# Softmax attention scores of a two-layer decoder: float32 products replaced by three products of high and low parts

## What is computed

```
qb = q.reshape(B, N, C, Hkv, G, d)              # C = 128 tokens, N = 4 blocks, d = 64
k2 = concatenate([previous key block, own key block])
scores = einsum('bnikgd,bnjkd->bkgnij', qb, k2) * d ** -0.5
logits = concatenate([where(band, scores, -inf), sink]); p = softmax(logits)
```

## Time and profile before

| | us |
|---|---|
| median of 3 runs | 2451.79 |
| lowest, highest run | 2450.35, 2451.99 |
| the profiled execution's own time | 2451.35 |
| its span in the trace | 2449.6 |

### The profile page before, as it was taken

The page is one execution under the profiler, slowest core; times in us unless marked ns, Lnnn a source line. Parts: engine busy times, 40 slices in busy tenths (PEclk is TensorE's granted clock), DMA queues, the critical chain, the costliest instruction groups (busy, mean ns, idle before and its releaser), DMA issues.

```text
span 2449.6 us, 33981 instructions
## 1 busy us (share of the span) xinstructions
PE 2422.6 (99%) x11352; PEld 1982.7 (81%) x11352; DVE 1477.2 (60%) x2263; ACT 869.6 (36%) x1359; POOL 210.5 (9%) x159
## 2 busy tenths in 40 slices
PE   7999999999999999999999999999999999999998
PEld 5888887877788888888888888787778888888887
DVE  3777779677744477433477677877775446533332
ACT  4222223555422342223332222345653223421232
POOL 0023012000003000010300000200100111000001
PEclk9999999999999999999999999999999999999999
DMA  7666664322235336443446566532222343332332
GB/s 265 191 191 189 189 182 142 97 69 60 67 103 148 103 112 197 121 123 104 116 120 191 178 197 198 164 118 80 67 60 78 112 147 102 93 109 82 98 103 82
DMA packets 505534, 315.20 MB, mean 129 GB/s; under 512 B 9256, under 2 KB 497016, under 8 KB 504824
## 3 DMA queue, kind: packets, MB, share of 16 engines
q1 hardware_dynamic: 437456, 246.86, 34.4%
q10 hardware_dynamic: 68008, 67.48, 8.8%
HBM read 308.02 MB, written 6.29 MB: 128 GB/s over the span
## 4 chain that ended last, share of the span: by engine, by line
PE 95%; DVE 3%; issue 1%; DMA 0%; ACT 0%; DVEq 0%; SPq 0%; ACTq 0%
PE ps_proj L1657 28%; PE ps_proj L1659 28%; PE ps_proj L1658 28%; PE ps_mid L1826 1%; PE ps_o L1844 1%; PE ps_mid L1874 1%; PE ps_mid L1875 1%; PE ps_mid L1876 1%; DVE sb_scratch L993 1%; PE ps_mid L1919 1%; PE ps_mid L1833 1%; DVE sb_w_lo L981 1%; PE ps_mid L1659 0%; PE ps_mid L1657 0%; PE ps_mid L1658 0%
## 5 line engine op out<-in xcount | busy, mean ns | idle before, releaser
L1657 PE MATMUL ps_proj<-sb_a_hi,sb_w_hi 128*128 128x512 f32 x1908 | 743.4, 390 | 4.9 <-DVE sb_w_lo L981 3.8
L1659 PE MATMUL ps_proj<-sb_a_hi,sb_w_lo 128*128 128x512 f32 x1908 | 742.4, 389 | 0.0
L1658 PE MATMUL ps_proj<-sb_a_lo,sb_w_hi 128*128 128x512 f32 x1908 | 742.4, 389 | 0.0
L592 ACT ACTIVATE sb_w_hi<-sb_raw 128x1024 fp32r<-128x1024 f32 (+1 forms) x388 | 430.9, 1111 | 833.7 <-PE ps_proj L1659 805.9
L981 DVE TENSOR_TENSOR sb_w_lo<-sb_raw,sb_w_hi 128x1024 fp32r<-128x1024 f32 (+1 forms) x388 | 506.3, 1305 | 311.3 <-ACT sb_w_hi L592 309.6
L1657 PE MATMUL ps_proj<-sb_h_hi,sb_w_hi 128*128 128x512 f32 x1212 | 478.9, 395 | 0.0
L1658 PE MATMUL ps_proj<-sb_h_lo,sb_w_hi 128*128 128x512 f32 x1212 | 472.0, 389 | 0.0
L1659 PE MATMUL ps_proj<-sb_h_hi,sb_w_lo 128*128 128x512 f32 x1212 | 471.9, 389 | 0.0
L1657 PEld LDWEIGHTS ps_proj<-sb_a_hi,sb_w_hi 128*128 128x128 f32 x1908 | 358.2, 188 | 81.5 <-issue 7.1
L1659 PEld LDWEIGHTS ps_proj<-sb_a_hi,sb_w_lo 128*128 128x128 f32 x1908 | 358.1, 188 | 74.9
L1658 PEld LDWEIGHTS ps_proj<-sb_a_lo,sb_w_hi 128*128 128x128 f32 x1908 | 358.3, 188 | 73.6
(11 more groups left out here) (231 smaller groups left out, 1797.8 us busy)
## 6 DMA issues: line engine op xcount, KB each, us to landing
sb_raw<-in_ffn_w_up SPq DMA_DIRECT2D x176, 512.0 KB, 3.8
sb_scratch<-in_w_ada ACTq DMA_DIRECT2D x128, 512.0 KB, 4.4
sb_raw<-in_w_in SPq DMA_DIRECT2D x100, 512.0 KB, 3.9
sb_raw<-in_ffn_w_down SPq DMA_DIRECT2D x64, 704.0 KB, 4.5
sb_raw<-in_w_branch_swa SPq DMA_DIRECT2D x16, 512.0 KB, 3.6
sb_raw<-in_w_branch_ret SPq DMA_DIRECT2D x16, 512.0 KB, 3.7
sb_raw<-in_w_out SPq DMA_DIRECT2D x16, 512.0 KB, 3.6
sb_scratch<-in_ffn_w_up SPq DMA_DIRECT2D x12, 512.0 KB, 6.5
```

What stands on the lines that cost most here:

```text
L592: act.activation(Whi[s][:, 0:n], raw[s][:, 0:n], ACT.Copy).then_inc(hi_ready, 1)
L1657: pe.matmul(bank, Whi[s][:, w], hi, start=first, stop=False)
L1658: pe.matmul(bank, Whi[s][:, w], lo, start=False, stop=False)
L1659: return pe.matmul(bank, Wlo[s][:, w], hi, start=False, stop=last)
```

## The change

It makes high and low parts of keys and of both query tiles, in the memory of `Ahi` and `Alo` that the head loop leaves free, and forms the scores of three products of them. The high part of the keys and the low part are made by POOL (two operations in the place of one copy), the high part of a query tile by ACT, the low part by DVE. PE waits for `query_lo` where it waited for `rope_done`.

```diff
-        k_cur = view(1280, 640)
+        k_parts, q_parts = zip(*((flat[:, 2304:2944], flat[:, 2944:3968].rearrange("p (s t) -> p s t", s=2))
+                                 for flat in (a.rearrange("p k t -> p (k t)") for a in (Ahi, Alo))))
...
 (POOL)
-                        pool.tensor_copy(k_cur, k_all[:, i // 2, :]).then_inc(key_in, 2)
+                        pool.tensor_copy(k_parts[0], k_all[:, i // 2, :]).then_inc(key_hi, 1)
+                        pool.wait_ge(key_hi, RH // 2 * l + i // 2 + 1)
+                        pool.sem_inc(carrier["pool"], 1)
+                        pool.tensor_tensor(k_parts[1], k_all[:, i // 2, :], k_parts[0].bitcast(F), ALU.subtract).then_inc(key_in, 2)
...
 (ACT)
+                def high_query(i, s):
+                    act.wait_ge(rope_done, LAYER_ROPES * l + 1 + 4 * i + s + 2)
+                    act.activation(q_parts[0][:, s, :], sq[:, s, :], ACT.Copy).then_inc(query_hi, 1)
...
-                def tail(i, start):
+                def tail(i, start, high=lambda s: None):
                     start(0)
                     decayed_hi(RH * l + i, 2)
+                    high(0)
                     start(1)
                     swa_out(2 * (RH * l + i) + 1, 2 * i + 1)
                     act.wait_ge(y_ps, RH * l + i + 2)
                     for e in range(2):
                         act.activation(probs[1][:, T * e:T * (e + 1)], pM[:, 2 + e, :], ACT.Square).then_inc(ysq, 1)
+                    high(1)
 
                 start_query(0, 0)
+                high_query(0, 0)
                 copy_own(4 * RH * l, 0, 0)
                 start_query(0, 1)
+                high_query(0, 1)
                 with act.Fori(0, RH - 1) as i:
                     middle(i)
-                    tail(i, lambda s: start_query(i + 1, s))
+                    tail(i, lambda s: start_query(i + 1, s), lambda s: high_query(i + 1, s))
...
 (DVE)
+                def low_query(i, s):
+                    dve.wait_ge(query_hi, 2 * numbers(i)[3] + s + 1)
+                    dve.tensor_tensor(q_parts[1][:, s, :], sq[:, s, :], q_parts[0][:, s, :].bitcast(F), ALU.subtract).then_inc(query_lo, 1)
...
                     decayed_lo(i, 2)
                     if next_head:
+                        low_query(i + 1, 0)
                         start_query(i + 1, 1)
...
                         dve.tensor_tensor(XV[:, 2 * i + e, :], pM[:, 2 + e, :], silu_g[:, e, :], ALU.mult).then_inc(y_free, 1)
+                    if next_head:
+                        low_query(i + 1, 1)
...
                 start_query(0, 0)
                 split_weights(b + 2, 0, UP_UNIT)
+                low_query(0, 0)
                 first_maxima(0)
                 start_query(0, 1)
                 split_weights(b + 2, 1, UP_UNIT)
+                low_query(0, 1)
                 normalise(4 * RH * l, 0)
...
 (PE)
-                    for a in range(2):
-                        p, first = slice(HD * a, HD * (a + 1)), 0 if blk else P
-                        last = pe.matmul(pM[:, a, 256 * n + first:256 * (n + 1)], sq[p, t, P * blk:P * (blk + 1)],
-                                         k_cur[p, P * blk + first:P * (blk + 2)], start=True, stop=True)
+                    for part, (of_q, of_k) in enumerate(((0, 0), (0, 1), (1, 0))):
+                        for a in range(2):
+                            p, first = slice(HD * a, HD * (a + 1)), 0 if blk else P
+                            last = pe.matmul(pM[:, a, 256 * n + first:256 * (n + 1)], q_parts[of_q][p, t, P * blk:P * (blk + 1)],
+                                             k_parts[of_k][p, P * blk + first:P * (blk + 2)], start=(part == 0), stop=(part == 2))
...
-                    pe.wait_ge(rope_done, rope0 + 2)
+                    pe.wait_ge(query_lo, 2 * n0 + 1)
...
-                    pe.wait_ge(rope_done, rope0 + 3)
+                    pe.wait_ge(query_lo, 2 * n0 + 2)
```

More of the change, by code:

```diff
@@ L239, in decoder @@
         swapped, rope_done = sem("swapped"), sem("rope_done")
+        key_hi, query_hi, query_lo = sem("key_hi"), sem("query_hi"), sem("query_lo")
         key_in, head_in, own_copied = sem("key_in"), sem("head_in"), sem("own_copied")
```

## The result

| | us |
|---|---|
| the changed kernel, median of 8 runs | 2458.49 (2458.22 to 2459.48) |
| the kernel before, median of 8 runs on the same chip | 2451.66 (2450.35 to 2451.99) |
| ratio, 95% interval | 1.0029 [1.0021, 1.0038] |
| span of the profiled execution, after and before | 2456.6 and 2449.6 |

A forecast was written before the change was run, and what follows sets the result against it. PE bounds the kernel (busy 99%). Per layer +1.83 us up to the third call, -1.05 (half = 1), +0.14 (half = 0), +0.30 (waits) make +1.22, in two layers +2.4: 2454.2 us, range 2450.5 to 2461.

The forecast's parts named there:

- rival 2: Score calls: short float32r products are no faster than float32, 0.213 us per 128-column pair; 2458.7 us, chance 0.17.
- Pace of the products: PE's score calls: pairs 0.118 us apart at 256 columns, 0.107 at 128; calls 0.91 us (half = 1), 0.88 (half = 0).
- Rivals 1: Score calls: the pass count rules, pairs of 0.107 and 0.053 us, calls 0.21 and 0.16 shorter; 2451.5 us, chance 0.13.
- The rule of four passes: Score calls: true FP32 makes four passes, so three products leave three quarters of the streaming, 0.64 and 0.48 us.
- the 0.21 us: End of each score call: drain before the next unit, 0.21 us, after streaming of 0.64 or 0.85 us.
- rival 3: Score calls: row halves do not run side by side in float32r, 12 steps instead of 6; 2474 us, chance 0.12.
- Waits of the first group: PE before the first and third call of each layer, for `query_lo` and DVE's L1278: 0.90 and 1.06 us.
- `low_query(i + 1, 1)` delays DVE by 0.6 us ... 0.88 of room, no wait: Third call of groups 1 to 3: DVE 0.6 us later, within 0.88 us of room, so no wait of PE.
- New end 526.40: a wait of 0.1 to 0.15: Transposes at the end of groups 0 to 2: ACT's copy delays POOL's L542; 0.1 us taken, three per layer.
- Costed at nothing: Tile 0's splits inside `tail` fall into idle time (otherwise 0.6 us each); POOL's extra subtraction, 1.6 us, is done before needed.

## Why the prediction was right or wrong

- **The sign and the class.** The forecast was +2.4 us, within 0.2%; measured is +6.8 us, just beyond. The range held the time, but by luck: the forecast by itself ended at 2456.5, and the part above it stood for rival 2, which did not happen: pairs of 128 columns are 0.11 us apart, not 0.21. That rival's 2458.7 is a coincidence.
- **Pace of the products: right.** 0.12 and 0.11 us per pair, calls of 0.90 and 0.89 us against 0.91 and 0.88. Rivals 1 and 3 are out as well. The rule of four passes would have given calls 0.21 and 0.16 us shorter; measured are 0.16 shorter and 0.03 longer. That fits the load of 128 columns as the limit of short products, but no run changes the load alone, so this reason is not shown.
- **Inside a call the 0.21 us were put in the wrong place.** I read the float32 call as three steps of 0.213 and then a long drain. Its single records start at 477.61, 477.93, 478.14 and 478.36, and the unit at 478.67: the first step has 0.1 us extra and the end has 0.1. The call after is built the same way (0.22 behind the first pair, 0.21 from the last pair to the unit), so the sum came out all the same. It also means that my sign for rival 3, a first step of 0.2 us, is there although the rival is not: twelve steps would have made the call 1.62 us.
- **Waits of the first group: right** in place, releaser and size (0.90 and 1.06 predicted; 0.93 and 1.03 measured). The table load starts 6.54 us after the first call (471.20 to 477.74) where it started 4.88 after it; with the call's own 0.93 that is 2.6 us later, 2.5 predicted. Both waits were taken away by the edits that this mechanism asks for.
- **"`low_query(i + 1, 1)` delays DVE by 0.6 us ... 0.88 of room, no wait": wrong, 2.85 us.** The price came from a group whose instructions ran while POOL was idle. Here POOL's L532 is under way, and the subtraction costs the queue 1.6 us. The earlier trace rows show POOL busy from 522.79 to 525.90, just where DVE gets a new instruction with two SBUF inputs. I looked at when POOL would be done, and not at what else runs beside it. What that costs also stood in the trace of the kernel before, outside the head loop: L1546, a subtraction of the same size, takes 0.69 us in 14 of its 16 places, and 2.31 in this one, 0.55 us past the end of POOL's instruction.

```profile
1938.93 1.90 POOL L506 TENSOR_TENSOR sb_scratch<-sb_scratch,sb_mod 128x1024 f32<-128x1024 f32 x1
...
1939.08 2.31 DVE L1546 TENSOR_TENSOR sb_a_lo<-sb_scratch,sb_a_hi 128x512 f32 x1 [0.90 <-ACT sb_a_hi L796]
```

- **"New end 526.40: a wait of 0.1 to 0.15": wrong in size, 2.4 us in place of 0.6.** ACT's shift of 0.5 us was right, and hidden when alone: in the run with ACT's copy only, POOL's sum ends 0.5 us later and the transposes come at most 0.04 us later in five of six places. I had held POOL's end against the first weight load, which runs 0.23 us ahead of the product. The sum also grew by 0.44 us from DVE's subtraction, and the two together made the wait of 0.36 us.
- **"Costed at nothing", tile 0 in the tail and POOL's key split: right**; no wait of PE names either.

With the two wrong steps put right the forecast's own sum comes out near the result: DVE's delay of 1.6 us less 0.88 of room less the 0.4 that PE is itself late there is 0.3, six times 2.0 us; the variance transposes at 0.4 and not 0.1 add 1.8; with the 2.4 of the forecast that is 6.2 us, against 6.8 measured.

## What to carry over

When work is added to DVE or POOL, price it by the other engine's timeline at that moment as well as by its own mean: here a DVE subtraction of 512 columns with two SBUF inputs that started under a POOL instruction lasted until that one's end plus 0.55 us, and held up POOL's next one in return. Look first for one group of equal shapes whose lengths spread in the profile before. Two additions that are each hidden or cheap alone can cost more than twice their sum: each used up most of the same room, and one moved the other engine's instruction onto the second. When a converted product brings new split work, the places of the splits in the engines' queues can be worth more than the products (6.6 us against 1.6 here), so these places are the first thing to move.

## What I had not expected of the hardware

- DVE and POOL wait for each other's whole instruction: 0.68 us became 1.16 to 1.70, by how early in POOL's instruction it started, and POOL's next went from 1.30 to 1.74 us; a POOL copy of 256 columns takes 0.94 us in place of 0.40 when it starts beside DVE's L1281.
- float32r products of 64 rows in two row halves run side by side like float32 ones, but the first step of a call is 0.22 us (477.80 to 478.02), 0.1 more than the following ones. The float32 call before had the same 0.1 (0.32 against 0.21).
- In the trace DVE's wait for POOL carries no releaser: it is inside the instruction's own length, and the row of DVE L1456 has no idle time. Only the spread of lengths within one group shows it.
